# A three-block transformer kernel: where the sigmoid of the gates is taken, and where attention splits its weights

## The reference, cut to what matters

```
proj = u @ w_in                                 # gate_a, gate_b: its last 2 x 1024 columns
o_a, o_b = attention(...)                       # second model: y_attn, y_rwkv
mix = sigmoid(gate_a) * (o_a @ w_branch_a) + sigmoid(gate_b) * (o_b @ w_branch_b)
h = h + mix @ w_out
```

## Time and profile before

| | us |
|---|---|
| median of 3 runs | 3024.78 (3020.69 to 3028.4) |
| the profiled execution | 3027.41 |
| its span, first to last instruction | 3026.1 |
| PE busy in the span | 2744.8 |
| ACT busy | 1227.2 |
| DVE busy | 1659.7 |

### The profile page before, as it was taken

One profiled execution on the slowest core, in us unless ns is written; L12 is line 12 of the kernel. 1 busy time (PEld: TensorE's weight loads), 2 busy tenths in 40 slices (PEclk: granted clock), 3 DMA queues, 4 the chain that ended last, 5 costly groups with the idle time before them and its releaser, 6 DMA issues.

```text
span 3026.1 us, 36544 instructions
## 1 busy us (share of the span) xinstructions
PE 2744.8 (91%) x14868; PEld 2052.7 (68%) x14868; DVE 1659.7 (55%) x2746; ACT 1227.2 (41%) x1800; POOL 118.8 (4%) x101
## 2 busy tenths in 40 slices
PE   6988899999998997889999999988989989689986
PEld 5766667888877775668788876666666668344445
DVE  3596445545445487545645455345443525477767
ACT  2217743423333225753424233244322312267765
POOL 0010000000000010000000000000000000022210
PEclk9999999999999899999999999899989889789998
DMA  3111232222221121223222222312111033389982
GB/s 116 64 62 63 79 110 91 98 98 97 90 91 60 56 70 60 77 74 132 84 98 98 98 85 82 112 41 79 43 45 66 23 119 125 141 295 392 382 335 97
DMA packets 64139, 334.93 MB, mean 111 GB/s; under 512 B 9568, under 2 KB 10336, under 8 KB 31072
## 3 DMA queue, kind: packets, MB, share of 16 engines
q1 hardware_dynamic: 58848, 324.14, 29.7%
q0 software_dynamic: 5120, 8.40, 0.9%
HBM read 312.58 MB, written 28.31 MB: 113 GB/s over the span
## 4 chain that ended last, share of the span: by engine, by line
PE 76%; DVE 11%; ACT 5%; DMA 4%; issue 3%; SPq 0%; POOL 0%; POOLq 0%; DVEq 0%; ACTq 0%
PE bank L888 14%; PE bank L890 14%; PE bank L889 14%; PE bank L1076 3%; PE bank L1077 2%; PE bank L1078 2%; PE bank L2274 2%; DMA hT<-in_WE 2%; ACT wh L1858 1%; DVE wl L1327 1%; PE bank L1120 1%; PE bank L2997 1%; PE bank L1148 1%; PE bank L1140 1%; PE bank L2983 1%
## 5 line engine op out<-in xcount | busy, mean ns | idle before, releaser
L888 PE MATMUL bank<-XH,wh 128*128 128x512 f32 x1312 | 528.6, 403 | 15.5 <-DVE XL L1368 11.5
L889 PE MATMUL bank<-XL,wh 128*128 128x512 f32 x1312 | 518.1, 395 | 0.0
L890 PE MATMUL bank<-XH,wl 128*128 128x512 f32 x1312 | 517.4, 394 | 0.0
L1327 DVE TENSOR_TENSOR wl<-raw,wh 128x2048 fp32r<-128x2048 f32 (+1 forms) x168 | 371.8, 2215 | 221.3 <-ACT wh L1858 221.1
L1858 ACT ACTIVATE wh<-raw 128x2048 fp32r<-128x2048 f32 (+1 forms) x168 | 309.0, 1842 | 190.0 <-DMA raw<-in_W 187.9
L888 PEld LDWEIGHTS bank<-XH,wh 128*128 128x128 f32 x1312 | 250.5, 191 | 93.9 <-issue 20.2
L890 PEld LDWEIGHTS bank<-XH,wl 128*128 128x128 f32 x1312 | 250.8, 191 | 53.6
L889 PEld LDWEIGHTS bank<-XL,wh 128*128 128x128 f32 x1312 | 251.1, 191 | 52.1 <-issue 2.4
L888 PE MATMUL bank<-arena_rounded,wh 128*128 128x512 f32 x576 | 231.1, 401 | 5.3 <-DVE arena_rounded L1572 3.2
L890 PE MATMUL bank<-arena_rounded,wl 128*128 128x512 f32 x576 | 230.0, 399 | 0.0
L889 PE MATMUL bank<-arena_rounded,wh 128*128 128x512 f32 x576 | 229.7, 399 | 0.0
(11 more groups left out here) (488 smaller groups left out, 4663.3 us busy)
## 6 DMA issues: line engine op xcount, KB each, us to landing
raw<-in_W SPq DMA_DIRECT2D x153, 1024.0 KB, 4.8
arena<-in_WE SPq DMA_DIRECT2D x56, 1024.0 KB, 9.9
hT<-in_WE SPq DMA_DIRECT2D x26, 1024.0 KB, 9.9
cst<-in_WE SPq DMA_DIRECT2D x14, 1024.0 KB, 10.0
gsave<-scr SPq DMA_DIRECT2D x48, 256.0 KB, 2.6
scr<-gsave SPq DMA_DIRECT2D x48, 256.0 KB, 3.9
raw<-in_W SPq DMA_DIRECT2D x8, 768.0 KB, 4.3
arena<-ytok SPq DMA_DIRECT2D x8, 512.0 KB, 7.4
```

What stands on the lines that cost most here:

```text
L888: pe.matmul(ps[0:c.stop - c.start, :], h[:, k, c], hi, start=i == 0, stop=False)
L889: pe.matmul(ps[0:c.stop - c.start, :], h[:, k, c], lo, start=False, stop=False)
L890: mm = pe.matmul(ps[0:c.stop - c.start, :], l[:, k, c], hi, start=False, stop=i == len(xs) - 1)
L1327: w_lo.inc(dve.tensor_tensor(wl[:, i % 3, 0:k], raw[:, i % 3, 0:k], wh[:, i % 3, 0:k].bitcast(F32), ALU.subtract), i)
```

## The change

`gate` no longer takes the sigmoid: it copies the tile, and the raw value goes to DRAM and back. A new function of ACT, `gates_on(m, t)`, takes the sigmoid of the two gate tiles of t in place in `GB`, one tile ahead of the branches' work; DVE waits for it (`gate_on`) and no longer for the read. In `attention`, ACT's cuts of step s move behind the exponential and the copy of the transposed job. DVE's cuts move behind `normalize`, one step later (`cuts_at(m, s - 1)`).

```diff
+        gate_on = Signal(sem("gate_on"), [(m, t, which) for m in range(3) for t in range(8) for which in range(2)])
...
             def attention(m, pick):            # DVE
                 todo = jobs[m]
                 for s in range(len(todo) + 6):
-                    for n in cuts_at(m, s):
-                        cuts_to(n)
...
                     if 0 <= s - 1 < len(todo):
                         normalize(m, s - 1)
+                    for n in cuts_at(m, s - 1):
+                        cuts_to(n)
...
-                    dve.wait_ge(*gate_r[4 * (j % 2) + i]((m, j, i)))
+                    dve.wait_ge(*gate_on((m, t, 0)))
...
-                    dve.wait_ge(*gate_r[4 * (j % 2) + 2 + i]((m, j, 2 + i)))
+                    dve.wait_ge(*gate_on((m, t, 1)))
...
-                bank.emptied(act.activation(gate_at(m, g), bank.ap(key), ACT.Sigmoid), key)
+                bank.emptied(act.activation(gate_at(m, g), bank.ap(key), ACT.Copy), key)
 
             def attention(m):                  # ACT
                 todo = jobs[m]
                 for s in range(len(todo) + 6):
-                    for n in cuts_at(m, s):
-                        cuts_to(n)
...
                         bank.emptied(act.activation(PT[(s - 2) % 2][:, 0:n], bank.ap(key)[:, 0:n], ACT.Copy), key)
+                    for n in cuts_at(m, s):
+                        cuts_to(n)
...
+            def gates_on(m, t):
+                j, i = divmod(t, 2)
+                for which in range(2):
+                    x = 2 * which + i
+                    act.wait_ge(*gate_r[4 * (j % 2) + x]((m, j, x)))
+                    s = GB[4 * (j % 2) + x]
+                    gate_on.inc(act.activation(s, s, ACT.Sigmoid), (m, t, which))
+
             def branches(m, n0):
+                gates_on(m, 0)
                 for t in range(8):
+                    if t < 7:
+                        gates_on(m, t + 1)
                     if t % 2:
                         cuts_to(n0 + t // 2 + 2)
                     high((("mix", m), t), t, MX[t % 2], mixed_o((m, t)))
```

## The result

The changed kernel takes 2979.6 us in the median of four runs (2970.47 to 2996.88), the kernel before, run beside it, 3026.59 (3020.69 to 3028.52). The ratio is 0.9854, its 95% interval 0.983 to 0.9878: 1.5% faster. Five more rounds gave 2984.99 and 0.9855 (0.9826 to 0.9884). The forecast was 2981.

A forecast was written before the change was run, and what follows sets the result against it. PE was taken as the bound, time won only where it idles or runs at low clock. 39.2 + 9.3 - 3.0 - 1.5 = 44.0 us off 3027.4 gave 2983.4, less 2.6 for the median: 2981 us, range 2968 to 3003.

The forecast's parts named there:

- Cuts in "b": Kind "b" attention steps, mixers 0 and 1: PE's waits for DVE's minimum shrink, 4.1 us plus 0.5 for reordering, per mixer.
- Cuts in "a": Kind "a" attention steps, mixers 0 and 1: PE's waits for ACT's transposed-tile copy shrink, gain 9.4 us a mixer (3 to 10.4).
- The root: Step 20 of kind "a" attention: PE's 2.9 us wait for a root shrinks, gain 1.4 us a mixer (0 to 2.9).
- The clock in attention: Kind "a" attention, mixers 0 and 1: fewer waits mean less low-clock time on PE, gain 4.2 us a mixer (0 to 5.3).
- Attention of mixer 2: Mixer 2's attention: shorter waits behind cuts and a better clock, gain 9.3 us (3 to 12.2).
- The recurrence: Heads of recurrence stages 1 to 3: a new table load on ACT delays the square, 3.0 us lost (0 to 3.9).
- A drain behind a load: Recurrence heads: by the skill page a switch costs 2.66 us with its drain, so three stages would lose 7.1 us.
- The branches: Branches: ACT's sigmoids and waits for gate reads delay DVE's tiles slightly, 1.5 us lost in all (0 to 4).
- half comes back: Attention: ACT's and DVE's moved cuts delay copies a step or two later, gain only 23 us, 3002 us; chance 0.18.
- the ring sets the pace: Attention: three score banks, DVE and ACT pace the steps, so waits reappear elsewhere, 3015 to 3025 us; chance 0.08.
- The fourth: Branches: gate reads land so late that ACT's wait reaches PE, slower, 3035 us; chance 0.04.
- more goes: Attention: nothing is left of the cut and root waits and the clock stays up, 55.6 us, 2969 us; chance 0.08.

The follow-up runs named there:

- dve_only: The changed kernel with ACT's cuts back at the head of their step, DVE's still moved: 2983.38 us, 0.9861 of the kernel before.
- gates_only: The changed kernel with both engines' cuts back at the head of their step, only the gates raw: 3031.19 us, 1.0009 of the kernel before.
- cuts_only: The kernel before with only the cuts of both engines moved, gates keeping their sigmoid in attention: 2979.07 us, 0.9862 of the kernel before.
- preload: The changed kernel plus three one-column sigmoids in ACT's idle time, loading the table ahead of recurrence stages 1 to 3: 2975.26 us, 0.9834 of before.
- gates_late: The changed kernel with the branches' sigmoids taken in their own turn, not one tile ahead: 2981.68 us, 0.9867 of the kernel before.
- again: The changed kernel unaltered, run once more: 2984.99 us, 0.9855 of the kernel before.
- head_double: The changed kernel plus a one-column sigmoid and exponential, two more table loads, at each head of recurrence stages 1 to 3: 2985.28 us, 0.987 of before.
- head_cut: preload with both engines' cut at the heads of recurrence stages 1 to 3 moved behind the work issued there: 2968.24 us, 0.982 of before.

## Why the prediction was right, and where it was not

**Cuts in "b".** Forecast 4.1 + 0.5 a mixer. In the whole attention of mixer 0 the waits of line 1120 for DVE and for `issue` were 5.9 + 7.6 us and are now 4.0 + 4.7, that is 4.8 less (the forecast had counted the waits for DVE, 5.9, alone). The three behind the cuts are gone; in the first steps a longer wait for DVE stands beside a shorter one for `issue`, as one does where only the order of the work changes.

**Cuts in "a".** Forecast: 12.0 falls to 2.6, and the trace has 2.8. The two waits of 0.8 us at the end of the stage (the drain) are part of it, as reckoned. The working priced the two moves together; `dve_only` shows that with DVE's made ACT's adds nothing.

**The root.** Forecast 1.4, measured 2.9 - 1.0 = 1.9. `gates_only` gives 1.4 of it (2.9 to 1.5), `cuts_only` 0.4 (2.9 to 2.5): the loads were the larger part.

**The clock in attention.** Forecast 4.2 a mixer. The waits fell by 4.8 + 9.2 + 1.9 = 15.9 us in mixer 0 and the stage by 20.4, so some 4.5 us are left for it, and "a" stands at 1.00. In mixer 1 PE's idle time fell by 14.8 us and the stage by 20.8, which leaves 6.0, above the bound of 5.3; there the time at 1.2 GHz fell from 24.3 to 10.3 us, in mixer 0 from 24.0 to 13.8.

**Attention of mixer 2.** Forecast 9.3, measured 8.8. The waits went from 10.4 to 4.5 us and the clock to 1.00.

**The recurrence.** The stop was sized rightly: 3 x 1.0 us forecast, 3.2 measured, at the wait that was named, by the load that was named, and `preload` took it away again. As the whole of what the stage pays the term was mis-sized: 3.0 forecast, 16.3 in the profiled execution. What the working left out is the clock. It had counted clock as a gain where waits go, in attention, and never as a loss where a wait is added. In that execution it was 16.3 - 3.2 = 13.1 us, with 121.8 us of the stage at 1.2 GHz against 82.6. It isn't paid in every execution: in `gates_late` the same program of the recurrence took 2.2 us more than before.

That the median came out at the forecast all the same is in part luck. The stretches with the same program were 8.5 us shorter, by their clock. And the profiled execution lies 7.5 us above the median of the runs, where before it lay 2.6 above. The four runs of this kernel spread over 26 us, and the six of `again` have their median at 2985.

**A drain behind a load.** The Trainium skill, "ScalarE: Activation LUTs", section "What ACT_TABLE_LOAD costs", would by the prediction's estimate make the three heads lose 7.1 us. The traces don't agree: they have 3.2 for three loads, and in `head_double` 9.0 for six loads and six small activations of some 0.2 us, 1.3 each for a load. A drain beyond the 1.28 us of the load isn't in these numbers.

**The branches.** Forecast 1.5 us, no more than 4. PE has no wait there that it had not before; the stage is 0.4 to 0.9 us longer with the clock at 0.96 to 1.00 from one execution to the next. The cover that was named was more than enough.

**The rivals.** The first, half comes back, needed waits one or two steps behind each cut. There are a few, and small: 1.2 us behind DVE's cut of step 19 in mixer 0, and 0.8 and 1.5 us behind two of the three cuts of mixer 2, where 1.5 was reckoned in all; behind the other cuts there are none. The third, the ring sets the pace, would have left attention's length: it fell by a tenth. The fourth needed reads landing after 15 us. The second, more goes, with 2969, is what `head_cut` reached, though with help that the change doesn't have.

## What to carry to other kernels

On an engine that works in order, put work that nobody wants yet behind the instruction that frees what another engine waits for, and look for the last link of the chain: of two engines' cuts in series, moving the second one past the first wanted instruction gave all of it, with the gates raw. Taking table loads out of one stage puts them where the next function is first used, so look for what stands there and call the table up with a one-column activation in idle time before. And where a few us of stops are traded, compare stage by stage: one kernel's executions differ here by more than the part that is under test.

## What the runs showed of the chip

A load of an ACT table took 1283 ns every time and the next instruction began right behind it; a one-column sigmoid placed ahead moved it into idle time, and PE's idle time in the recurrence was back near before's (44.6 us against 44.3, and 46.4 with the loads at the heads).

The clock's lower stretches in the recurrence were 13.7 us long or shorter in before and in every kernel without a load at the heads, but the longest was 17 to 44 us in seven of eight executions with one. One program of the recurrence had 44.4, 37.5 or 13.7 us of it, and took from 420 to 438 us. And `head_double`, with nearly four times the added stops, lost less to the clock than the full change. None of this was expected, and its rule stays open.
